# One encoder layer with product-key expert retrieval on one core: scores of two token tiles computed by quarters among the query slabs

## What is computed

```python
q = jnp.einsum('td,de->te', x, wq).reshape(T, PEER_HEADS, 2, PEER_DHALF)
s = jnp.einsum('thcd,hcnd->thcn', q, keys).astype(jnp.float32)
v1, i1 = lax.top_k(s[:, :, 0], PEER_TOPK)
v2, i2 = lax.top_k(s[:, :, 1], PEER_TOPK)
...
top_s, pos = lax.top_k(cand, PEER_TOPK)
idx = jnp.take_along_axis(cidx, pos, axis=-1).reshape(T, PEER_HEADS * PEER_TOPK)
g = jax.nn.softmax(top_s, axis=-1).reshape(T, PEER_HEADS * PEER_TOPK)
...
a = jnp.einsum('td,tkd->tk', xt, u_tab[it])
hid = (jax.nn.gelu(a.astype(jnp.float32), approximate=False) * gt).astype(xt.dtype)
return jnp.einsum('tk,tkd->td', hid, v_tab[it])
```

## Time and profile before

| | |
|---|---|
| median of 3 runs | 3742.63 us (3737.31 to 3744.31) |
| the profiled execution | 3735.37 us, its span 3733.6 us |
| DVE busy | 2762.9 us (74%) |
| PE busy | 2471.0 us (66%) |
| DMA, mean | 357 GB/s, 1332.43 MB |
| granted TensorE clock, mean | 0.82 |

### The profile page before, as it was taken

The page is one execution under the profiler, slowest core; times in us unless marked ns, Lnnn a source line. Parts: engine busy times, 40 slices in busy tenths (PEclk is TensorE's granted clock), DMA queues, the critical chain, the costliest instruction groups (busy, mean ns, idle before and its releaser), DMA issues.

```text
span 3733.6 us, 30440 instructions
## 1 busy us (share of the span) xinstructions
PE 2471.0 (66%) x11208; PEld 1892.2 (51%) x11208; DVE 2762.9 (74%) x3210; ACT 332.7 (9%) x832; POOL 1246.5 (33%) x1273
## 2 busy tenths in 40 slices
PE   7798799978975777959988999999978000000000
PEld 7687689545743444535677877777767000000000
DVE  5331220979989997787789889976655999988888
ACT  1212311000002221000100000000000000000000
POOL 2420000122233332223222223232222577777772
PEclk9899899988986657989999999999999555555555
DMA  8774355898998999989999999999998999999998
GB/s 245 219 232 121 143 190 179 292 397 332 341 405 343 406 419 375 422 343 414 421 422 423 423 423 423 423 421 424 423 382 336 413 407 410 409 390 370 392 373 348
DMA packets 297908, 1332.43 MB, mean 357 GB/s; under 512 B 70752, under 2 KB 136832, under 8 KB 146336
## 3 DMA queue, kind: packets, MB, share of 16 engines
q0 software_dynamic: 138624, 945.22, 62.9%
q1 hardware_dynamic: 126400, 371.83, 26.7%
q10 hardware_dynamic: 32736, 13.44, 1.4%
HBM read 1282.60 MB, written 57.20 MB: 359 GB/s over the span
## 4 chain that ended last, share of the span: by engine, by line
PE 35%; DMA 27%; DVE 22%; POOL 8%; issue 6%; another core or an unknown queue 1%; ACT 1%; ACTq 1%; SPq 0%; DVEq 0%; POOLq 0%
PE low L1559 18%; DMA arena<-in_ut 16%; PE low L1900 10%; DVE arena L1375 7%; DVE acc L1391 5%; DMA arena<-in_peer_v,arena 5%; POOL arena L611 4%; POOL arena L620 4%; DMA arena<-in_w 2%; DMA arena<-in_peer_u,arena 2%; PE low L1633 1%; PE acc L1633 1%; DMA arena<-y_scratch_b 1%; DVE low L1391 1%
## 5 line engine op out<-in xcount | busy, mean ns | idle before, releaser
L1391 DVE SCALAR_TENSOR_TENSOR acc<-arena,acc 128x2048 f32<-128x2048 f32 x443 | 1042.6, 2354 | 262.4 <-DMA arena<-in_peer_v,arena 226.7
L1559 PE MATMUL low<-arena 128*128 128x192 f32 (+1 forms) x4096 | 1064.8, 420 | 100.6 <-DMA arena<-in_w 77.3
L1900 PE MATMUL low<-arena 128*128 128x256 f32 x4096 | 915.5, 383 | 110.1 <-DMA arena<-in_ut 109.0
L1559 PEld LDWEIGHTS low<-arena 128*128 128x128 f32 x4096 | 738.3, 196 | 376.0 <-DMA arena<-in_w 74.6
L1900 PEld LDWEIGHTS low<-arena 128*128 128x128 f32 x4096 | 774.1, 191 | 251.3 <-DMA arena<-in_ut 133.2
L611 POOL DMA_INDIRECT arena<-in_peer_v,arena x576 | 579.5, 1006 | 924.3 <-DVE acc L1391 772.6
L1375 DVE SCALAR_TENSOR_TENSOR arena<-arena,acc 128x2048 f32<-128x2048 f32 x320 | 724.8, 2284 | 115.3 <-DMA arena<-in_peer_u,arena 107.6
L611 POOL DMA_INDIRECT arena<-in_peer_u,arena x320 | 320.1, 1000 | 1185.6 <-DVE arena L1375 856.1
L1391 DVE SCALAR_TENSOR_TENSOR low<-arena,low 128x2048 f32<-128x2048 f32 x126 | 296.6, 2354 | 35.8 <-DMA arena<-in_peer_v,arena 26.8
L620 POOL DMA_INDIRECT arena<-expert_scratch,arena x256 | 263.3, 1029 | 83.2 <-issue 83.2
L872 ACT COPY arena<-low 128x256 f32<-128x256 f32 x128 | 47.6, 372 | 971.0 <-PE low L1900 957.9
(11 more groups left out here) (274 smaller groups left out, 1678.3 us busy)
## 6 DMA issues: line engine op xcount, KB each, us to landing
arena<-in_w SPq DMA_DIRECT2D x128, 1024.0 KB
arena<-in_ut SPq DMA_DIRECT2D x128, 1024.0 KB
expert_scratch<-arena SPq DMA_DIRECT2D x128, 128.0 KB
arena<-in_peer_v,arena POOLq DMA_INDIRECT x576
arena<-toeplitz_scratch SPq DMA_DIRECT2D x64, 128.0 KB, 3.6
arena<-c_scratch SPq DMA_DIRECT2D x64, 128.0 KB, 4.2
bias_scratch<-distance_scratch SPq DMA_DIRECT2D x1, 5120.0 KB, 23.4
x_scratch<-arena ACTq DMA_DIRECT2D x5, 1024.0 KB
```

What stands on the lines that cost most here:

```text
L1391: stt(held, slot[j], wv_, held, ALU.mult, ALU.add).then_inc(used, 1)
L1559: ins = mm(L[n % 2][:, 0:width], wring[n % 2][:, k, :], rhs(k), start=k == 0, stop=k == KT - 1)
L1900: ins = mm(L[j % 4][:, 0:NSD], ud[j % 4][:, k, :], lane(catB, k)[:, P:NB], start=k == 0, stop=k == KT - 1)
```

## The change

1. **Scores by quarters.** The scores of tile 0 and of tile 2 are no longer computed after the 16th query slab of their group. PE computes a quarter (`quarter`, four matmuls into `L[2]` or `L[3]`) inside slabs 4, 8 and 12, after five of their 16 matmuls, and the fourth quarter after the last slab. ACT copies each out. A new semaphore `quarter_out` counts them.
2. **Heads among the slabs.** DVE waits for a quarter and then chooses and decodes its two heads. In tile 0 the eight heads stand without rows between them, and 56 rows follow where 14 rows between heads and 28 rows after them stood. In tile 2 the order is 11 rows, and then four times 9 rows and two heads; before, it was 53 rows, eight times 5 rows and a head, and `decode` with 6 rows. Tile 2 now is decoded head by head (`decode_head`).
3. **Slots.** Slots 2 and 3 may be used from row 2 on instead of row 16. Gathers into them still wait for all heads of tile 0. POOL waits for single heads of tile 2 as it did for tile 0 (`chosen` gives the count of `idx_ready`).
4. **Loads of the first sums one at a time.** The five loads of `early_sums` go ahead of blocks 93, 99, 105, 111 and 117, one each, instead of all ahead of block 117. The wait for the last tile's experts moves with the first of them.
5. **Square root for tile 0** of the second layer norm: after block 121 instead of block 125 in ACT's order.

```diff
-SLOT_FROM = [0, 0, TOPK, TOPK, STEPS[0] + 6, R_U2 + 16]
+SLOT_FROM = [0, 0, 2, 2, STEPS[0] + 6, R_U2 + 16]
...
+def chosen(t, h=PH - 1):
+    return {0: h + 1, 1: PH + 1, 2: PH + 2 + h, 3: 2 * PH + 2, 4: 2 * PH + 3}[t]
...
             def early_sums():
-                sp.wait_ge(idx_ready, PH + NT - 1)
+                sp.wait_ge(idx_ready, chosen(NT - 1))
                 sp.wait_ge(v_stored, 32)
                 sp.dma_start(x1f[0], x1scr[0]).then_inc(early_in, 16)
+                yield
                 sp.dma_start(vsum[0], vscr[0]).then_inc(early_in, 16)
+                yield
...
-                if j == EB - 12:
-                    early_sums()
+                if j in range(EB - 36, EB - 11, 6):
+                    next(sums)
...
+            def quarter(t, c):
+                act.wait_ge(score_done, 4 * t + c + 1)
+                if t == NGA and not c:
+                    act.wait_ge(x1_stored, 16 * NT)
+                ins = nc.scalar.copy(scored[t][:, 512 * c:512 * c + 512], L[2 + c % 2])
+                ins.then_inc(quarter_out, 1)
...
-            products(106, EB - 2)
+            products(106, EB - 6)
             ln2(0, 0)
-            products(EB - 2, EB)
+            products(EB - 6, EB)
...
-            dve.wait_ge(score_out, 1)
             for h in range(PH):
+                if h % 2 == 0:
+                    dve.wait_ge(quarter_out, h // 2 + 1)
                 head(0, h)
                 decode_head(0, h)
-                if h:
-                    rows(2)
             logits(0)
             link.zero()
-            rows(28)
+            rows(56)
...
-            rows(53)
+            rows(11)
             dve.wait_ge(keys_in, 48)
-            dve.wait_ge(score_out, 3)
             for h in range(PH):
-                rows(5)
+                if h % 2 == 0:
+                    rows(9)
+                    dve.wait_ge(quarter_out, 4 + h // 2 + 1)
                 head(2, h)
-            decode(2, rows)
+                decode_head(2, h)
+            logits(2)
+            link.zero()
             rows_to(R_U2 + 4)
...
+            def quarter(t, c, qp, base, keys):
+                first = (N_WA, N_WB)[t // 2]
+                c0 = MIXCOL[t] - base
+                pe.wait_ge(slab_out, first + 4 * c + 4)
+                pe.wait_ge(keys_in, 32 + 16 * (t // 2))
+                if c >= 2:
+                    pe.wait_ge(quarter_out, 4 * (t // 2) + c - 1)
+                for q in range(4):
+                    ins = mm(L[2 + c % 2][:, P * q:P * q + P], qp[:, 4 * c + q, c0:c0 + P],
+                             keys[:, P * (4 * c + q):P * (4 * c + q) + P], start=True, stop=True)
+                ins.then_inc(score_done, 1)
```

More of the change, by code:

```diff
@@ L532, in early_sums @@
             def early_sums():
-                sp.wait_ge(idx_ready, PH + NT - 1)
+                sp.wait_ge(idx_ready, chosen(NT - 1))
                 sp.wait_ge(v_stored, 32)
                 sp.dma_start(x1f[0], x1scr[0]).then_inc(early_in, 16)
+                yield
                 sp.dma_start(vsum[0], vscr[0]).then_inc(early_in, 16)
+                yield
                 sp.dma_start(x1f[1][0:TS], x1scr[1, 0:TS, :]).then_inc(early_in, 16)
+                yield
                 sp.dma_start(vsum[1][0:TS], vscr[1, 0:TS, :]).then_inc(early_in, 16)
+                yield
                 sp.dma_start(vsum[2][0:TS], vscr[1, TS:P, :]).then_inc(early_in, 16)
+                yield
+            sums = early_sums()
             for j in range(EB):
@@ L595, in gather @@
                     if s % TOPK == 0:
-                        pool.wait_ge(idx_ready, s // TOPK + 1)
+                        pool.wait_ge(idx_ready, chosen(0, s // TOPK))
+                elif kind == "u" and t == 2:
+                    if s % TOPK == 0:
+                        pool.wait_ge(idx_ready, chosen(2, s // TOPK))
                 elif s == 0 and kind == "u" or i == R_V3 or i == R_V4:
-                    pool.wait_ge(idx_ready, PH + t)
+                    pool.wait_ge(idx_ready, chosen(t))
                 if before is not None:
@@ L880, in mixed_a @@
                 for i in range(16):
+                    if first == N_WA and i and i % 4 == 0:
+                        quarter(0, i // 4 - 1)
                     act.wait_ge(slab_done, first + i + 1)
@@ L897, in _ @@
             mixed_a(N_WA)
-            scores(0)
+            quarter(0, 3)
             scores(1)
@@ L999, in _ @@
             ln1_out(4)
-            slabs_out(N_WB, 16, mixB, NB)
-            for t in range(NGA, NT):
+            for i in range(16):
+                if i and i % 4 == 0:
+                    quarter(2, i // 4 - 1)
+                out_of(N_WB + i, mixB[:, i, :], L[i % 2][:, 0:NB])
+            quarter(2, 3)
+            for t in range(NGU, NT):
                 scores(t)
@@ L1760, in scores @@
                 c0 = MIXCOL[t] - base
-                if t:
+                if t > 1:
                     pe.wait_ge(score_out, t)
@@ L1767, in scores, with queries, between @@
                     ins.then_inc(score_done, 1)
+            def quarter(t, c, qp, base, keys):
[9 more added lines that the diff above has]
+                ins.then_inc(score_done, 1)
+            def queries(i, t, qp, base, keys):
+                def between(k):
+                    if k == 4 and i and i % 4 == 0:
+                        quarter(t, i // 4 - 1, qp, base, keys)
+                return between
             ca, cb = (lambda k: lane(catA, k)), (lambda k: lane(catB, k))
@@ L1782, in _ @@
             pe.wait_ge(x1t_out, 8)
+            pe.wait_ge(res_ready, 2)
             for i in range(16):
[L1784 to L1788, removed]
+                slab(N_WA + i, ca, NA, queries(i, 0, mixA, 0, keysA))
+            quarter(0, 3, mixA, 0, keysA)
             scores(1, mixA, 0, keysA, acc)
@@ L1888, in _ @@
             for i in range(16):
[L1889 to L1892, removed]
+                slab(N_WB + i, cb, NB, queries(i, 2, mixB, NA, keysB))
+            quarter(2, 3, mixB, NA, keysB)
+            for t in range(NGU, NT):
                 scores(t, mixB, NA, keysB, low)
```

8 lines of the change are left out of this document (5 added, 3 removed).

## The result

| | time, us (median; range) | against the kernel before | span of the profiled execution |
|---|---|---|---|
| before | 3740.49; 3737.31 to 3744.31 | | 3733.6 |
| after | 3820.82; 3820.35 to 3822.01 | 1.0215, 95% 1.0197 to 1.0232 | 3818.7 |

The account below looks back on a forecast made before the run. DVE and DMA are full with expert rows, and rows from 587 begin only when the expert products end. Terms +8 + 1 - 7 - 2 = 0 on 3735.4 us; against the median 3742 us, range 3722 to 3762.

Parts of the forecast that it names:

- 56 rows instead of 42 before the scan: At group B's scan: 56 rows, paced by DMA, delay the scan and PE at 921 us by +8 us, bounds 0 and +18.
- its rival: Slower case: before the scan, gathers sharing 16 engines delay `u`'s stores and moves PE needs; +17 us, 3757 us, chance 0.26.
- the single loads: Blocks 92 to 127: taking the five loads of the first sums apart gives -7 us, ends 0 and -20.
- the square root: At the last block: tile 0's root made earlier lets tile 1's follow the block at once, -2 us.
- The advice to interleave regimes: Interleave regimes with different bounds, done twice here; cited for a rival keeping 14 rows' lead, 3704 us, chance 0.03.
- Heads of tile 0 among the slabs: Before tile 0's first row: seven heads, 70 us of DVE, move under PE's slabs at no cost to PE.
- Heads of tile 2 among the slabs: In group B's slabs: eight heads done at about 1903 us with row 342, DMA idling where full; costed at nothing.
- the lead of 14 rows: DVE's advance from 56 less 42 rows, held at group B's last layer norm, 1683.2 us, forecast gone at 1867 us.
- the gate: DVE's wait at rows 583 to 586 for ACT's roots, 24.68 us to spare; row 587 on begins when expert products end.
- Scores: Group B: quarters put 2.9 us into slabs, take out 3.84, plus one copy wait; +1 us, between -1 and +2.
- SP's moved wait: SP's wait for the last experts, moved from ahead of block 117 to block 93: 115 us of room, costs nothing.
- The tail: From row 586 to the end: pace unchanged; the prediction called itself wrong if the tail changed its pace.

Follow-up runs that it names:

- e8: First group's part alone on the kernel before, with POOL waiting ahead of row 4 for the moves of `u` and 38 rows before the scan: 3710.20 us, ratio 0.9986.
- e9: First group's part alone on the kernel before, POOL's wait for the moves cut in three (rows 4, 8, 12), 38 rows: 3732.89 us, ratio 0.9980.
- e5: Kernel before with only the second group's quarters and heads of tile 2 among the slabs, 67 rows ahead of them: 3738.08 us, ratio 1.0057.
- e6: As e5, but 5 rows, head, 4 rows, head in place of 9 rows and two heads: 3724.01 us, ratio 1.0019.
- e3: The whole change with POOL waiting ahead of row 4 for the moves of `u`, and 38 rows in place of 56: 3748.59 us, ratio 1.0082.
- e12: The changed kernel with e8's wait and 38 rows, e6's order of heads, square root after block 121, five loads in one pile: 3752.05 us, ratio 1.0039.
- e2: Kernel before with all of the change but its first group's part: 3747.09 us, ratio 1.0084.
- e7: First group's part alone on the kernel before, with POOL waiting for the moves of `u` ahead of row 20, and 44 rows: 3724.34 us, ratio 1.0025.
- e1: Kernel before with only the first group's part of the change (slots, tile 0's quarters and heads, 56 rows): 3792.79 us, ratio 1.0200.
- e4: Kernel before with only the loads of the first sums taken apart, one each: 3715.97 us, ratio 0.9997.

## Why the prediction was wrong

**The step that failed** is "56 rows instead of 42 before the scan", +8 us at the scan. For DVE's rows its working came out: the first row at 667.3 us (forecast 664), row 55 worked at 849.6 to 851.9 us (the text had 859, by its bounds of 0 and +18 from 847.5 to 866). But it made DVE's rows the thing that ends last at the scan, and PE's pairs were taken to stand still. The copy came at 924.8 us, +77.4 in place of +8, since ACT copied the scan's last pair only then. The text had the cause in its rival ("the stores of `u` and its many small moves that PE needs for the scan", and "PE's scan pairs later than now" as the deciding point) and priced it at +18, from bytes: it took the many small packets off the spare of the gathers, 1 or 2 rows, and did not ask what the gathers take off the packets. The 32 moves have 48 KB each in pieces of 192 bytes, 256 packets each and 8192 together. By an estimate from the 2007 turns in 50 us they need some 200 us beside the gathers; by their bytes, 1.5 MB at the 413 GB/s of the earlier trace rows, 4 us. From the first issue to the end of the last it was 159 us (680.8 to 839.5). The gathers' queue had gaps too: in 805 to 810 us q10 has 678 packets beside 224, in 800 to 805 us they are again alike, 245 and 244. A view of the queues by packets in 690 to 740 us of the kernel before, 7034 against 950, could have warned ahead of the run.

**The whole sum** at row 586, forecast and measured: the scan +8, measured +77.4; from there to the first expert block +1, measured +1.9; from the first block to block 92 nothing, measured +5.3, for which no run shows a cause; the single loads in blocks 92 to 127 -7, measured +3.4; the square root -2, measured -2.5 (the second division stands 0.6 us behind the last block's copy, before 3.1). This makes 85.5, of which the first term is nine tenths.

**The rule** cited for the single loads, that each DMA engine goes round its queues packet by packet (the Trainium skill, "DMA: Bandwidth & Descriptors", queues, rings and completion order), was used for two queues with like packets, and not for the one pair of queues where it decides. The equal counts, 2007 and 2007, 1537 and 1537, agree with it. In the profile's counts a turn is one piece of 8192 bytes on the one side and one piece of 192 bytes on the other. The advice to interleave regimes (the Trainium skill, "Perfetto Trace Analysis", optimization strategy), by which the change should have gained, says that performance may improve. As made, the change lost 80 us. With the gathers held back, the first interleaving gained 5 and 7 us (e8, e9). The second alone lost 21 and 7 us (e5, e6).

**Heads of tile 0 among the slabs**, at no cost to PE: right within 3 us. Row 0 came at 667.3 us (before 664.7), with eight heads done.

**Heads of tile 2 among the slabs**, costed at nothing: right in the changed kernel. Everything there is shifted by the 77.4 us of the scan. With that taken off, DVE is 14 rows ahead at the last layer norm and level at 1867 us, row 342 comes at 1902 us (forecast 1903), and row 388 at 2074.2 against 2074.3 before. DMA fell under 400 GB/s, as forecast (297 in 1831 to 1944 us). But the term hung on the lead of 14 rows. e5, where the heads stand at the same row without the lead, has row 388 53 us late and row 580 46, and the cover that the text had named (24.68 us at the gate, "that cover would be gone, us for us") is used up. The lead also goes where the gathers are held back, since 38 rows then stand where the change has 56: e3 is +30 and e12 +15, and e8, without these heads among the slabs, is -5. So the term held, but only with the lead, and the prediction had no price for the case without it. That bytes not moved in a full stretch are missing until the next wait that has room is how I read e5; no run varies it by itself.

**Scores**, +1: the first block in the changed kernel is 79.3 us late with the copy 77.4 late, so +2, within its ends. All of group B's other work lies between the two as well, so this bounds the term and does not isolate it.

**Single loads**, -7 (0 to -20): measured -1 with an interval of -5 to +3, so -7 is out and 0, the upper end of the range, is in. **Square root**, -2: no run of its own, but -2.5 in the changed kernel by the two divisions above. **SP's moved wait**, nothing: right. Even in e2, where tile 4 is decoded 65 us later than before (2513.4 us), SP issues block 92 and the first single load in its usual step (2573.26 and 2574.17 us).

**The tail** from row 586 on kept its pace in the change (3801.7 - 2981.1 = 820.6 us, before 820.9), so all is decided ahead of the gate, as the text said.

## What to carry to other kernels

Before gathers or other large transfers are moved into a stretch, count the packets of every other queue that is active there, not its bytes: here small packets beside a queue that never ran empty went at the large ones' rate (40 a us in place of 400), and the engine that issued them stood still with all its compute. Where DMA is full, a long piece of vector work between rows cost bytes (e5, +21 us), unless the vector engine had a lead to spend, as in the changed kernel. And a wait that swallows delays is one budget for all parts of a change: parts that are nearly free by themselves (-5 and +7 us) need not be together (+15). If one part of a change gives the lead that another spends, a repair of the first has to be priced for both.

## What was not expected of the hardware

- Two queues with equal numbers of packets, as by one each in turn: 2007 and 2007 in 50 us, 1537 and 1537 in 40 us, with mean sizes of 7.3 KB and 180 bytes, and three queues with 666, 664 and 665 in 15 us. The small ones took 4.1% of the engines' time and made 40 a us. With the gathers' queue empty or nearly so, 4082 (e7, 740 to 750 us) and 4333 (e3, 716 to 726 us) went in ten us.
- An engine that issues DMAs can be held by them: one of the small moves took 0.34 to 0.8 us to issue where they went through at once (e3), and 22 of the 32 took 2.2 to 12.5 us beside the gathers (the changed kernel). The sixth of the first burst is the first slow one (5.9 us). ACT's copies, 0.48 us each, stood behind up to 69.8 us of issues. What limit an issue runs into, no view shows.
- Chips can differ in one stretch and not in the rest: from row 586 to the end 814 to 818 us (e1 to e8) against 835 to 839 (before, after, e9 to e12), with row 580 within 3 us (e4 and before).
